# Two-layer encoder trunk on one core: neighbourhood-attention outputs laid out by features, with divided probabilities as the moving operand

## The chip, the core and the metric

The kernel runs on one core of a Trainium2 chip. The metric is device microseconds (us) of one execution of the whole program. A core has a matrix engine (TensorE, PE in the profile, with its weight loads as PEld), a vector engine (VectorE, DVE), a scalar engine (ScalarE, ACT), GpSimd (POOL) and a queue engine (SyncE, SP) that issues the transfers. The engines run at the same time, each in the order of its own program, and wait for each other through semaphores only.

## The reference

Two layers over 256 tokens of 1024 features. Each layer adds three parts to the residual: a mixer, a cross-attention into 256 memory tokens, and a gated convolutional feed-forward; each starts with an RMS norm. The change concerns the mixer and its output projection:

```python
proj = h @ w_in                         # q, k, v and gates of three groups of heads
ml_out = head_rms_norm(ml_h, ml_norm_g, ML_HEADS) * sigmoid(ml_o)      # 6 mLSTM heads
# 5 neighbourhood heads: 256 tokens on a 4 x 64 grid, window of 16 columns, all rows
s = einsum('brqhd,brkwhd->bhrqkw', qg, k_band) * d ** -0.5 + bias
s = where(in_win, s, -inf)
p = softmax(s)
o = einsum('bhrqkw,brkwhd->brqhd', p, v_band)
gla_out = head_rms_norm(gla_h, gla_norm_g, GLA_HEADS) * silu(g_g)      # 5 gated linear heads
return concatenate([ml_out, na_out, gla_out], axis=-1) @ w_out
```

Every head has 64 features. So of the 1024 mixed features, 384 come from mLSTM, 320 from the neighbourhood heads and 320 from gated linear attention (GLA). In blocks of 128 features (k = 0 to 7), blocks 0, 1 and 2 are mLSTM, 3 and 4 are neighbourhood, block 5 is half neighbourhood and half GLA, 6 and 7 are GLA.

## The kernel before, in words

Tokens lie on partitions in two tiles of 128 (`t`), features in eight blocks of 128 (`k`). All large products are made of three products of two parts: each weight and activation is split into an upper part (`whi`, `xhi`, `yhi`, written by ScalarE) and a lower part (`wlo`, `xlo`, `ylo`, written by VectorE), and `split_mm` (lines 663 to 667) issues upper by upper, upper by lower and lower by upper. Weights come in units of 1 MB or less through a ring of three slots: SP loads a unit into `raw` when the lower part of the unit three before it is done, ScalarE copies the upper part (`split_hi`, line 1096), VectorE subtracts for the lower part (`split_lo`, line 1455), and TensorE waits for it (`have`). Each engine takes the units in the one order of `layer_units`, at the places in its program where a `split_hi` or `split_lo` stands.

PSUM has eight banks. `layer_events` writes out by hand in which order TensorE fills which bank (`job`), and `layer_drains` in which order ScalarE and VectorE empty them. `free(name)` on TensorE waits until the job that had the bank before has been drained.

The neighbourhood stage is the loop over `hh` in 0 to 6, written three times, once in the program of each engine. For a head n:

- `nas`: TensorE multiplies queries by keys into a bank (line 882). Heads come in pairs (0, 1), (2, 3) at hh = 0 and 2, head 4 alone at hh = 4; the two heads of a pair lie in the two halves of the partitions.
- VectorE adds the bias with the window mask, negated, and takes the extreme of each row (line 1624), into `np_[:, n % 2]`.
- ScalarE takes the exponential, with the row sum in `nsum` (line 1262), and counts up `np_ready`.
- `nat`: one step later, TensorE waits for `np_ready` and transposes the four 128x128 blocks (line 864); ScalarE copies them to `npt[:, n % 2]` (line 1249).
- `nao`: again one step later, TensorE multiplies: the transposed exponentials stand, the 64 values of the head move, four products per head, tokens on the output partitions (line 872). VectorE inverts the row sums (line 1611) and scales the outputs by them into `tmb` (line 1614).

Between these, TensorE has fills: `gg` (gates of GLA) at hh = 0, then the cross-attention's key blocks `xk0` to `xk3`, two halves each (`NA_FILL`). In layer 1 two of the four key blocks are made elsewhere, so its fills are half as long. Each key block needs its split, and the first of them the eight upper and lower parts of the memory. VectorE's program of this loop also holds: the sum of the mLSTM heads over their two directions with its denominators (lines 1632 to 1638), the key splits, the products of GLA's queries and keys with their decays (lines 1646, 1647, 1655), the squares of the mLSTM heads (1588, 1589) and the split of `xv0a`.

Behind the loop comes GLA: `kt0` and `kt1` (turns of decayed keys, lines 900 and 904), `ga`, `kv`, then the memory's values `xv0`, `go` and `xv1a`. When `tmb` holds all mixed heads (`mixed_ready`), TensorE transposes the eight blocks (`mx_0` to `mx_3`, two blocks each, line 978), ScalarE and VectorE split them into `yhi` and `ylo` with the gains (lines 1301 and 1710), and TensorE makes the output projection (`wo0`, `wo1`), for each half unit first token tile 0, then tile 1. Token tile rows within the neighbourhood heads' blocks are stored in reversed order inside each grid row, and `mixed_parts` names which pieces of a block must be read backwards.

## Time and profile before

| | us |
|---|---|
| median of 3 runs | 879.58 |
| lowest and highest of them | 879.28, 880.8 |
| profiled execution, its time | 878.24 |
| profiled execution, its span | 876.3 |
| TensorE busy in the span | 861.8 |
| VectorE busy in the span | 596.0 |
| ScalarE busy in the span | 496.1 |

The span is that of the instructions on the core; the time also has what lies around it, 1.94 us here. Rows of a timeline give the start, the duration, the engine and line, the operands by name (arena is a region that holds the stages' temporaries, bank is PSUM) and how many like instructions are merged in the row. A bracket at the end says how long the engine stood idle before and what released it. Matrix products overlap: the next starts before the one before ends, so the step between starts is what one costs. A product of full 32-bit operands shows as two records, a transpose as one.

### The profile page before, as it was taken

The page shows a single profiled execution, that of the slowest core. Times are in us where ns is not written, and L with a number is a line of the kernel's source. Part 1 is how long each engine was busy: PE and PEld are TensorE (multiplying, and loading weights), DVE is VectorE, ACT ScalarE, POOL GpSimd, SP SyncE. Part 2 cuts the span into 40 slices and gives each one's busy share as a digit, 9 for nine tenths or more (in the row PEclk, how much of TensorE's full clock was granted, in tenths as well). Part 3 has the DMA queues.
Part 4 walks back from the last instruction along what each step waited for, and adds up shares of the span by engine and source line. Part 5 has one row for each costly group of instructions (what it writes and reads, how often), then busy time and mean ns, then how long its engine had stood idle before and what let it go on. Part 6 is the DMA issues. An engine that isn't in the chain of part 4 may idle for free.

```text
span 876.3 us, 14948 instructions
## 1 busy us (share of the span) xinstructions
PE 861.8 (98%) x6338; PEld 798.1 (91%) x6338; DVE 596.0 (68%) x820; ACT 496.1 (57%) x689; POOL 14.3 (2%) x35
## 2 busy tenths in 40 slices
PE   8999999999999999999999999999999899999997
PEld 8999998889889999999999999988898899999996
DVE  6887678757657666666577885887665666656655
ACT  7954663658647445445567546745755645445444
POOL 5000000000000000000000000000000000000000
PEclk9999999999999999999999999999999999999999
DMA  9735452364255555555448254335435365555541
GB/s 329 201 102 177 156 178 103 112 226 144 97 193 190 195 190 195 192 191 194 145 140 257 72 171 165 127 115 192 135 109 191 127 212 190 193 196 190 192 169 48
DMA packets 114665, 146.78 MB, mean 168 GB/s; under 512 B 10600, under 2 KB 94760, under 8 KB 114600
## 3 DMA queue, kind: packets, MB, share of 16 engines
q1 hardware_dynamic: 114456, 145.57, 49.7%
q8 instruction: 50, 0.82, 0.4%
q10 hardware_dynamic: 144, 0.26, 0.1%
q14 instruction: 15, 0.12, 0.0%
HBM read 144.77 MB, written 1.05 MB: 166 GB/s over the span
## 4 chain that ended last, share of the span: by engine, by line
PE 92%; ACT 3%; DVE 3%; issue 1%; DMA 0%; ACTq 0%; DVEq 0%
PE bank L665 26%; PE bank L666 25%; PE bank L667 25%; PE bank L706 4%; PE bank L743 2%; PE bank L832 2%; DVE wlo L1455 2%; PE bank L1017 2%; ACT whi L1096 1%; ACT yhi L1119 1%; PE bank L872 1%; PE bank L762 1%; PE bank L849 1%; DVE ylo L1710 1%; PE bank L882 1%
## 5 line engine op out<-in xcount | busy, mean ns | idle before, releaser
L1455 DVE TENSOR_TENSOR wlo<-raw,whi 128x2048 fp32r<-128x2048 f32 (+3 forms) x144 | 306.2, 2133 | 106.1 <-ACT whi L1096 105.2
L1096 ACT ACTIVATE whi<-raw 128x2048 fp32r<-128x2048 f32 (+3 forms) x144 | 257.4, 1793 | 53.5 <-PE bank L667 48.4
L665 PE MATMUL bank<-yhi,whi 128*128 128x256 f32 x704 | 195.1, 277 | 0.5 <-DVE ylo L1471 0.5
L666 PE MATMUL bank<-ylo,whi 128*128 128x256 f32 x704 | 194.6, 276 | 0.0
L667 PE MATMUL bank<-yhi,wlo 128*128 128x256 f32 x704 | 194.6, 276 | 0.0
L665 PEld LDWEIGHTS bank<-yhi,whi 128*128 128x128 f32 x704 | 132.2, 188 | 1.6 <-issue 0.7
L666 PEld LDWEIGHTS bank<-ylo,whi 128*128 128x128 f32 x704 | 132.2, 188 | 0.8
L667 PEld LDWEIGHTS bank<-yhi,wlo 128*128 128x128 f32 x704 | 132.2, 188 | 0.0
L665 PE MATMUL bank<-xhi,whi 128*128 128x256 f32 x320 | 91.4, 286 | 2.2 <-DVE wlo L1455 1.2
L665 PE MATMUL bank<-whi,xhi 128*128 128x512 f32 (+2 forms) x256 | 90.1, 352 | 0.0
L667 PE MATMUL bank<-xhi,wlo 128*128 128x256 f32 x320 | 88.9, 278 | 0.0
L666 PE MATMUL bank<-xlo,whi 128*128 128x256 f32 x320 | 88.8, 278 | 0.0
L667 PE MATMUL bank<-whi,xlo 128*128 128x512 f32 (+2 forms) x256 | 88.5, 346 | 0.0
L666 PE MATMUL bank<-wlo,xhi 128*128 128x512 f32 (+2 forms) x256 | 88.5, 346 | 0.0
L666 PE MATMUL bank<-wlo,fhi 128*128 128x512 f32 x176 | 69.0, 392 | 0.0
L665 PE MATMUL bank<-whi,fhi 128*128 128x512 f32 x176 | 68.9, 391 | 0.0
L667 PE MATMUL bank<-whi,flo 128*128 128x512 f32 x176 | 68.6, 390 | 0.0
L665 PEld LDWEIGHTS bank<-xhi,whi 128*128 128x128 f32 x320 | 60.3, 188 | 7.1 <-issue 5.2
L1395 ACT ACTIVATE arena<-bank,pcols 128x256 f32<-128x256 f32 x44 | 22.4, 561 | 67.1 <-PE bank L667 67.1
L667 PEld LDWEIGHTS bank<-xhi,wlo 128*128 128x128 f32 x320 | 60.1, 188 | 0.0
L666 PEld LDWEIGHTS bank<-xlo,whi 128*128 128x128 f32 x320 | 60.1, 188 | 0.0
L665 PEld LDWEIGHTS bank<-whi,xhi 128*128 128x128 f32 x256 | 48.1, 188 | 5.1 <-issue 1.3
(268 smaller groups left out, 1373.1 us busy)
## 6 DMA issues: line engine op xcount, KB each, us to landing
raw<-in_w_up SPq DMA_DIRECT2D x44, 1024.0 KB, 5.0
raw<-in_w_down SPq DMA_DIRECT2D x22, 1024.0 KB, 4.8
raw<-in_w_in SPq DMA_DIRECT2D x10, 1024.0 KB, 7.3
raw<-in_w_xk SPq DMA_DIRECT2D x8, 1024.0 KB, 5.1
raw<-in_w_xv SPq DMA_DIRECT2D x8, 1024.0 KB, 4.9
raw<-in_w_out SPq DMA_DIRECT2D x8, 1024.0 KB, 4.8
raw<-in_w_xq SPq DMA_DIRECT2D x8, 1024.0 KB, 5.7
raw<-in_w_xo SPq DMA_DIRECT2D x8, 1024.0 KB, 4.9
```

The lines of the kernel that those rows point to most:

```text
L665: mm(o, s_hi, m_hi, start=first, stop=False, skip_group_check=True)
L666: mm(o, s_hi, m_lo, start=False, stop=False, skip_group_check=True)
L667: return mm(o, s_lo, m_hi, start=False, stop=last, skip_group_check=True)
L706: last = mm(bank(name, 2, T)[:, f, :], w[:, k, f * P:f * P + P], x[:, k, :], start=k + i + f == 0, stop=k == KT - 1 and i == 2, skip_group ...
L743: last = mm(bank(names[t])[:, 0:n], x[:, k, t * P:(t + 1) * P], w[:, k, :], start=k + i == 0, stop=False, skip_group_check=True)
L762: last = nc.tensor.transpose(turned_bank(l, group, k)[:, t * P:(t + 1) * P], tmb[:, t, k * P:(k + 1) * P], ident[:])
L832: last = mm(o[:, t, d, :], w[:, c:c + P], mv[:, jt, g, :], start=i == 0, stop=i == len(src) - 1)
L849: last = mm(bank(f"mls{hh + x}", TT, T)[:, jt, :], qk[r, 3 + j, jt * P:(jt + 1) * P], qk[r, j, :], start=True, stop=True)
L1017: last = mm(bank(f"xo_{hh}", 2, T)[:, f, :], xv[:, jt, hh * XD + f * P:hh * XD + (f + 1) * P], xpt[:, hh, jt, :], start=jt == 0, stop=jt == 1)
L1096: A(weight(whi, gu), raw[:, gu % RING, 0:SIZE[gu]], ACT.Copy).then_inc(hi_done, 1)
L1395: last = A(fy[:, p % 2, f, :], bank(f"fa{p}", 2, T)[:, f, :], ACT.Identity, scale=pcol[:, RA + RB_W + 22 + j:RA + RB_W + 23 + j], bias=pco ...
L1455: tt(weight(wlo, gu), raw[:, gu % RING, 0:SIZE[gu]], weight(whi, gu), ALU.subtract).then_inc(lo_done, 1)
```

## The change

The neighbourhood outputs are computed with features on the partitions. The 64 values of a head stand and the transposed probabilities of all 256 queries move, two products per head. The heads of a pair (`NA_PAIRS`: 0 with 1, 2 with 3, 4 alone) go to the two halves of one bank's partitions. Outputs are made at three places instead of five (`NA_OUT`, hh = 3, 5, 6), before the turn of that step.

Since queries now lie along the free dimension, the division by the row sums can no longer be done on the outputs. VectorE divides the exponentials in `np_` itself (`shares_of`), between ScalarE's exponential and TensorE's turn, and the turn waits for a new semaphore `npn_ready`. The outputs are already turned, so they are split at once: ScalarE copies the upper part to `yna_hi`, VectorE subtracts for `yna_lo` (`heads_lo`); these arrays lie where the neighbourhood queries and keys were. The transposes of blocks 3 and 4 before the output projection go, and `yhi` and `ylo` are formed for six blocks instead of nine pieces (`MIXED_K`; of block 5 only its GLA half). The output projection starts with block 3 for both token tiles, then blocks 0, 1, 2, then the rest.

On VectorE the order inside the loop changes: the mLSTM head sums move from hh = 0 to hh = 2 (before the divisions of heads 2 and 3 in layer 0, behind them in layer 1), the GLA products stand behind the divisions, the split of the second key block (`xk1` in layer 0, `xk3` in layer 1) moves into hh = 0. On ScalarE that block's upper part moves before the draining of `gg1`, and the two GLA exponentials move behind the exponentials of heads 2 and 3. The drain of `nao2` stands behind those of `kt0` and `kt1`. The core of the diff:

```diff
+        if h in NA_OUT:
+            p = NA_OUT.index(h)
+            job(f"nao{p}", 4 + p % 2)
...
-        if h >= 2:
-            job(f"nao{h - 2}", 4 + (h - 2) % 2)
...
+NA_OUT = (3, 5, 6)
+NA_PAIRS = ((0, 1), (2, 3), (4,))
+NA_K = range(3, 6)
...
                 for hh in range(NAH + 2):
+                    if hh in NA_OUT:
+                        p = NA_OUT.index(hh)
+                        is_drained(pe, l, f"nat{NA_PAIRS[p][-1]}")
+                        free(f"nao{p}")
+                        for jt in range(TT):
+                            for g in NA_PAIRS[p]:
+                                r = slice(64 * (g % 2), 64 * (g % 2) + 64)
+                                last = mm(bank(f"nao{p}")[r, 0:T], nav[:, jt, g * DH:(g + 1) * DH], npt[:, g % 2, jt].rearrange("p a b -> p (a b)"),
+                                          start=jt == 0, stop=jt == 1, skip_group_check=True)
+                        last.then_inc(te_done, 1)
                     if 1 <= hh <= NAH:
                         g = hh - 1
-                        pe.wait_ge(np_ready, NAH * l + g + 1)
+                        pe.wait_ge(npn_ready, NAH * l + g + 1)
                         free(f"nat{g}")
...
                             for jt in range(TT):
-                                last = nc.tensor.transpose(bank(f"nat{g}", TT, TT, P)[:, t, jt, :], np_[:, g % 2, t, jt * P:(jt + 1) * P], ident[:])
-                        last.then_inc(te_done, 1)
-                    if hh >= 2:
-                        g = hh - 2
-                        is_drained(pe, l, f"nat{g}")
-                        free(f"nao{g}")
-                        for t in range(TT):
-                            for jt in range(TT):
-                                last = mm(bank(f"nao{g}")[:, t * DH:(t + 1) * DH], npt[:, g % 2, t, jt, :],
-                                          nav[:, jt, g * DH:(g + 1) * DH], start=jt == 0, stop=jt == 1)
+                                last = nc.tensor.transpose(bank(f"nat{g}", TT, TT, P)[:, jt, t, :], np_[:, g % 2, t, jt * P:(jt + 1) * P], ident[:])
                         last.then_inc(te_done, 1)
...
                     for k in (i, i + 4):
+                        if k not in MIXED_K:
+                            continue
                         for t in range(TT):
...
                     last.then_inc(te_done, 1)
-                for n in range(2):
-                    tm_unit(f"wo{n}", (f"wo{n}0", f"wo{n}1"), 512, "mx", n == 0)
+                tm_half("wo0", "a", ("wo00", "wo01"), 512, "mx", True, ks=(3,), first=3, ends=None)
+                tm_half("wo0", "a", ("wo00", "wo01"), 512, "mx", True, ks=(0, 1, 2), first=3, ends=2)
+                tm_half("wo0", "b", ("wo00", "wo01"), 512, "mx", True)
+                tm_unit("wo1", ("wo10", "wo11"), 512, "mx")
...
                 for hh in range(NAH + 2):
+                    if hh in NA_OUT:
+                        p = NA_OUT.index(hh)
+                        r = slice(0, 64 * len(NA_PAIRS[p]))
+                        is_filled(act, l, f"nao{p}")
+                        A(forwards(yna_hi[r, p, :]), backwards(bank(f"nao{p}")[r, 0:T]), ACT.Copy).then_inc(na_hi_ready, 1)
                     if 1 <= hh <= NAH:
...
                         drain(A(npt[:, (hh - 1) % 2].rearrange("p a b c -> p (a b c)"), bank(f"nat{hh - 1}"), ACT.Copy))
-                    if hh == 1:
-                        if l == 0:
-                            split_hi("xk1")
-                        else:
-                            split_hi("xk3")
-                        act.wait_ge(bc_ready, l + 1)
-                        A(b1[:], zc, ACT.Exp, scale=1.0 / 16).then_inc(eb_ready, 1)
-                        A(b3[:], zc, ACT.Exp, scale=-1.0 / 16).then_inc(eb_ready, 1)
                     if hh < NAH and hh % 2 == 0:
...
                             last.then_inc(np_ready, 1)
+                    if hh == 2:
+                        act.wait_ge(bc_ready, l + 1)
+                        A(b1[:], zc, ACT.Exp, scale=1.0 / 16).then_inc(eb_ready, 1)
+                        A(b3[:], zc, ACT.Exp, scale=-1.0 / 16).then_inc(eb_ready, 1)
                     if hh == 0:
...
+                        split_hi("xk3" if l else "xk1")
...
                 split_hi("wo0b")
-                for k in range(KT):
+                for k in MIXED_K:
                     is_filled(act, l, f"mx_{k % 4}")
-                    if k >= 4:
+                    if k - 4 in MIXED_K:
                         lo_is(act, l, "mx", k - 4)
-                    for r, v in mixed_parts(k):
-                        last = A(forwards(yhi[r, k, :]), v(turned_bank(l, "mx", k)[r, :]), ACT.Copy, scale=pcol[r, R_MG + k:R_MG + k + 1])
-                    last.then_inc(xhi_ready, 1)
+                    r, hi, _ = mixed(k)
+                    A(hi, turned_bank(l, "mx", k)[r, :], ACT.Copy, scale=pcol[r, R_MG + k:R_MG + k + 1]).then_inc(xhi_ready, 3 if k == 5 else 1)
                 split_hi("wo1b")
...
+                def heads_sum():
+                    is_drained(dve, l, f"mlo{MLH - 1}")
+                    dve.wait_ge(em_ready, l + 1)
+                    hr = hraw[:].rearrange("p t d h e -> p (t d h) e")
+                    link(stt(den[:, :], hr[:, :, DH], -1.0, hr[:, :, DH], ALU.mult, ALU.max))
+                    link(tt(den[:, :], den[:, :], em[:].rearrange("p t d h -> p (t d h)"), ALU.max))
+                    link(V.reciprocal(den[:, :], den[:, :]))
+                    link(tt(hr[:, :, 0:DH], hr[:, :, 0:DH], den[:].rearrange("p (n o) -> p n o", o=1).broadcast_to([P, 24, DH]), ALU.mult))
+                    link(tt(mlh, hraw[:, :, 0, :, 0:DH], hraw[:, :, 1, :, 0:DH], ALU.add))
+                def shares_of(g):
+                    dve.wait_ge(np_ready, NAH * l + g + 1)
+                    link(V.reciprocal(nsum[:, 2 * g:2 * g + 2], nsum[:, 2 * g:2 * g + 2]))
+                    for t in range(TT):
+                        last = ts(np_[:, g % 2, t, :], np_[:, g % 2, t, :], nsum[:, 2 * g + t:2 * g + t + 1], None, ALU.mult)
+                    last.then_inc(npn_ready, 1)
+                def heads_lo(p):
+                    dve.wait_ge(na_hi_ready, 3 * l + p + 1)
+                    r = slice(0, 64 * len(NA_PAIRS[p]))
+                    drain(tt(forwards(yna_lo[r, p, :]), backwards(bank(f"nao{p}")[r, 0:T]), forwards(yna_hi[r, p, :]), ALU.subtract))
                 for hh in range(NAH + 2):
-                    if hh == 2:
-                        dve.wait_ge(eb_ready, 2 * l + 2)
-                    if hh >= 2:
-                        g = hh - 2
-                        dve.wait_ge(np_ready, NAH * l + g + 1)
-                        link(V.reciprocal(nsum[:, 2 * g:2 * g + 2], nsum[:, 2 * g:2 * g + 2]))
-                        is_filled(dve, l, f"nao{g}")
-                        for t in range(TT):
-                            last = ts(tmb[:, t, ML + g * DH:ML + (g + 1) * DH], bank(f"nao{g}")[:, t * DH:(t + 1) * DH],
-                                      nsum[:, 2 * g + t:2 * g + t + 1], None, ALU.mult)
-                        drain(last)
                     if hh < NAH and hh % 2 == 0:
...
                         split_lo("ggb")
-                        is_drained(dve, l, f"mlo{MLH - 1}")
-                        dve.wait_ge(em_ready, l + 1)
-                        hr = hraw[:].rearrange("p t d h e -> p (t d h) e")
-                        link(stt(den[:, :], hr[:, :, DH], -1.0, hr[:, :, DH], ALU.mult, ALU.max))
-                        link(tt(den[:, :], den[:, :], em[:].rearrange("p t d h -> p (t d h)"), ALU.max))
-                        link(V.reciprocal(den[:, :], den[:, :]))
+                        for g in NA_PAIRS[0]:
+                            shares_of(g)
                         split_lo("xk2" if l else "xk0")
                         memory_lo("mem", l, range(KT))
-                        link(tt(hr[:, :, 0:DH], hr[:, :, 0:DH], den[:].rearrange("p (n o) -> p n o", o=1).broadcast_to([P, 24, DH]), ALU.mult))
-                        link(tt(mlh, hraw[:, :, 0, :, 0:DH], hraw[:, :, 1, :, 0:DH], ALU.add))
-                    if hh == 1 and l == 0:
-                        split_lo("xk1")
+                        split_lo("xk3" if l else "xk1")
                     if hh == 2:
+                        if l == 0:
+                            heads_sum()
+                        for g in NA_PAIRS[1]:
+                            shares_of(g)
                         if l:
-                            split_lo("xk3")
+                            heads_sum()
+                        else:
+                            split_lo("xk2")
+                        dve.wait_ge(eb_ready, 2 * l + 2)
                         is_drained(dve, l, "gk")
...
                         link(ins)
-                        if l == 0:
-                            split_lo("xk2")
                     if hh == 3:
...
                             split_lo("xk3")
+                        heads_lo(0)
                     if hh == 4 and l == 0:
...
                     if hh == 4:
+                        shares_of(4)
                         split_lo("xv0a")
-                    if hh == 5 and l:
-                        head_squares(mlh, sq, 0, MLH)
+                    if hh == 5:
+                        if l:
+                            head_squares(mlh, sq, 0, MLH)
+                        heads_lo(1)
                 is_filled(dve, l, "kt0")
...
                 drain(V.tensor_copy(kty[:].rearrange("p a b c -> p (a b) c"), bank("kt1", 4, P)[:, :, 0:32]))
+                heads_lo(2)
                 for i in range(4):
```

Not shown: the order of drains, which follows the above, the allocations, and `tm_half`, which gets the arguments `first` and `ends` and takes its inputs from `operand`, that is from `yna_hi` and `yna_lo` for blocks 3 to 5.

## Rows read from the trace of the kernel before

**Rows 1.** The page: busy time of each engine; granted clock in 40 slices

```profile
PE 861.8 (98%) x6338; PEld 798.1 (91%) x6338; DVE 596.0 (68%) x820; ACT 496.1 (57%) x689; POOL 14.3 (2%) x35
...
PEclk9999999999999999999999999999999999999999
```

**Rows 2.** Timeline of VectorE, layer 1: start us, us, line, names, count [idle before]

```profile
542.44 0.19 DVE L1632 SCALAR_TENSOR_TENSOR den<-arena 128x24 f32<-128x24 f32 x1
...
544.45 2.29 DVE L1455 TENSOR_TENSOR wlo<-raw,whi 128x2048 fp32r<-128x2048 f32 x1 [1.26 <-ACT whi L1096]
...
549.83 1.75 DVE L1637 TENSOR_TENSOR arena<-arena,den 128x1536 f32<-128x1536 f32 x1
...
553.40 0.17 DVE L1611 RECIPROCAL nsum<-nsum 128x2 f32<-128x2 f32 x1 [0.83 <-ACT arena L1257]
...
554.00 0.41 DVE L1624 CUSTOM_DVE_ANT_0 arena<-bank,bt 128x256 f32<-128x256 f32 x1
...
555.38 2.29 DVE L1455 TENSOR_TENSOR wlo<-raw,whi 128x2048 fp32r<-128x2048 f32 x1
...
557.58 0.68 DVE L1646 TENSOR_TENSOR arena<-gq,arena 128x512 f32<-128x512 f32 x1
...
560.10 0.17 DVE L1611 RECIPROCAL nsum<-nsum 128x2 f32<-128x2 f32 x1
...
560.69 1.28 DVE L1655 TENSOR_TENSOR arena<-arena 128x512 f32<-128x512 f32 x2
...
567.25 0.95 DVE L1588 TENSOR_TENSOR qk<-qk 128x768 f32<-128x768 f32 x1
...
569.10 0.15 DVE L1611 RECIPROCAL nsum<-nsum 128x2 f32<-128x2 f32 x1
```

**Rows 3.** Timeline of TensorE, layer 0, neighbourhood stage, in the same columns

```profile
114.25 1.00 PE L872 MATMUL bank<-nav,arena 128*128 128x64 f32 x8
115.18 1.13 PE L882 MATMUL bank<-nak,naq 64*128 64x256 f32 x8
116.25 0.38 PE L665 MATMUL bank<-xhi,whi 128*128 128x256 f32 x1
...
122.44 1.00 PE L872 MATMUL bank<-nav,arena 128*128 128x64 f32 x8
123.26 0.36 PE L665 MATMUL bank<-xhi,whi 128*128 128x256 f32 x1
...
130.18 1.13 PE L882 MATMUL bank<-nak,naq 64*128 64x256 f32 x4
131.24 0.38 PE L665 MATMUL bank<-xhi,whi 128*128 128x256 f32 x1
```

**Rows 4.** Timeline of TensorE, layer 0, carried GLA products

```profile
152.28 1.52 PE L956 MATMUL bank<-arena 128*64 128x256 f32 x12
```

**Rows 5.** Timeline of TensorE, layer 0, turning of the mixed heads and output projection

```profile
165.00 1.91 PE L978 MATMUL bank<-ident,tmb 128*128 128x128 f32 x16
166.77 0.47 PE L665 MATMUL bank<-whi,yhi 128*128 128x512 f32 x1
...
172.09 0.39 PE L667 MATMUL bank<-whi,ylo 128*128 128x512 f32 x1
172.79 0.50 PE L665 MATMUL bank<-whi,yhi 128*128 128x512 f32 x1 [0.32 <-DVE wlo L1455]
```

**Rows 6.** Timeline of VectorE, layer 0, one division of the cross-attention

```profile
217.70 0.62 DVE L1746 TENSOR_SCALAR tmb<-tmb,nsum 128x256 f32<-128x256 f32 x2
```

**Rows 7.** Timeline of ScalarE, layer 1, neighbourhood stage

```profile
546.79 1.71 ACT L1124 ACTIVATE xhi<-memT,pcols 128x256 fp32r<-128x256 f32 x4 [0.19 <-PE bank L667]
...
549.51 1.91 ACT L1096 ACTIVATE whi<-raw 128x2048 fp32r<-128x2048 f32 x1
...
554.80 0.51 ACT L1262 ACTIVATE arena<-arena,nmax 128x256 f32<-128x256 f32 x1 [1.00 <-DVE nmax L1624]
```

**Rows 8.** Timeline of TensorE, layer 1, first GLA turn

```profile
568.18 0.61 PE L900 MATMUL bank<-ident,arena 128*128 128x128 f32 x4
```

More of the change, by code:

```diff
@@ L521, in forwards, with operand, mixed @@
             return v.rearrange("p (r c) -> p r c", c=GW)
-        def mixed_parts(k):
-            lo, hi = k * P, k * P + P
-            return [(slice(max(lo, a) - lo, min(hi, b) - lo), v)
-                    for a, b, v in ((0, ML, forwards), (ML, ML + NA, backwards), (ML + NA, DM, forwards)) if max(lo, a) < min(hi, b)]
+        def operand(group, k):
+            if group == "mx" and k in NA_K:
+                return yna_hi[:, k - 3, :], yna_lo[:, k - 3, :]
+            return tuple(x[:, k, :] for x in PAIR[group])
+        def mixed(k):
+            r = slice(64, P) if k == 5 else slice(0, P)
+            return (r,) + tuple(x[r] for x in operand("mx", k))
+        MIXED_K = (0, 1, 2, 5, 6, 7)
         block = ctx.enter_context(nc.Block())
@@ L1706, in _ @@
                 split_lo("wo0a")
-                for k in range(KT):
+                for k in MIXED_K:
                     hi_is(dve, l, "mx", k)
-                    for r, v in mixed_parts(k):
-                        last = stt(forwards(ylo[r, k, :]), v(turned_bank(l, "mx", k)[r, :]), pcol[r, R_MG + k:R_MG + k + 1],
-                                   forwards(yhi[r, k, :]), ALU.mult, ALU.subtract)
-                    last.then_inc(xlo_ready, 1)
+                    r, hi, lo = mixed(k)
+                    stt(lo, turned_bank(l, "mx", k)[r, :], pcol[r, R_MG + k:R_MG + k + 1], hi, ALU.mult, ALU.subtract
+                        ).then_inc(xlo_ready, 3 if k == 5 else 1)
                 split_lo("wo1b")
```

32 lines of the change are left out of this document (22 added, 10 removed).

## The prediction

> **What bounds the kernel now.** I read the first part of the profile page first: TensorE is busy for 861.8 of 876.3 us, VectorE for 68% and ScalarE for 57% [rows 1]. TensorE sets the time almost everywhere, so the change is worth what it takes from TensorE's own work, less every wait that it puts in front of TensorE. The granted clock is at its upper level, 2.4 GHz, in all 40 slices [rows 1]. Then I read the timelines of TensorE, VectorE and ScalarE through the neighbourhood stage of both layers (about 99 to 139 us and 538 to 568 us) and through the turning of the mixed heads behind it, looking at start times: matmuls are pipelined, so the step from one start to the next is the price, not the duration printed. The reader should see in them that TensorE goes from group to group without a gap while VectorE has only small ones: in layer 1 its work runs through with one idle of 1.26 and one of 0.83 in 16 us [rows 2]. VectorE is thus the second limit of this stage, and the change lengthens just the chain that runs through it.
>
> **Change, TensorE's work.** A head's outputs now cost 0.93 or 0.82 us (114.25 to 115.18, 122.44 to 123.26), five heads per layer [rows 3]: 4.3 us at 0.86 each. The new form makes two pairs and a single head, 256 columns moving, 64 features stationary, the heads of a pair in the two halves of the output partitions. The nearest rows are the score products: two heads of 256 columns in the two row halves take 1.07 us (115.18 to 116.25), and one head alone takes 1.06 (130.18 to 131.24), so halves run beside each other and a single head wastes one [rows 3]. The carried GLA products have exactly the new form, halves alternating: 12 records in 1.52 us, or (1.52 - 0.38)/11 = 0.104 each, 0.83 for eight [rows 4]. Bounds for a pair are 0.83 below and 2 x 1.06 = 2.12 above (no overlap). I take 1.07, since those eight records enter and leave the half-array form once each, as a pair will. Per layer: 2 x 1.07 + 1.06 = 3.2, a saving of 1.1 if nothing waits.
>
> The Trainium skill (TensorEngine Tiling, Key Properties) says that changing the tiling mode drains the engine, and the change adds such switches. It agrees with the single head's 1.06 for four records; by that rule 0.83 is too low and 1.07 stands. By the same page's advice to swap the operands and tile the columns (When to Use Tiling) the products would halve, to about 2.2 us per layer, an estimate that would take 1 us more per layer if no wait came instead.
>
> **Change, turning and output projection.** Four of 16 transposes go per layer; 16 take 166.77 - 165.00 = 1.77 us, so 0.44 goes [rows 5]. Then TensorE waits at the second half of `wo0`: the last record of the first half starts at 172.09, steps there are 0.23, but the next starts at 172.79 behind a `wlo` split, 0.47 late [rows 5]. VectorE can only begin that split after its nine `ylo` operations; six remain, about 0.4 each (as the 256-column steps in [rows 2]), so it comes 1.2 earlier plus what the earlier first transposes give, against a TensorE that comes 0.44 earlier. The wait goes. The six products of k = 3 that now come first have inputs ready long before and cover the turn of k = 0. In layer 1 the same pattern stands; I take the same. Saving 0.91 per layer, 1.82 in all. Less ScalarE work there (nine `yhi` become six) is hidden as now.
>
> **Change, the wait that is added.** The turn of a head (`nat`) waited for its exponentials; it now waits until VectorE has divided them. A division is a reciprocal (0.2 to the next start) and two scalings of 128x256, which take 0.62 together in the cross-attention [rows 6]: 0.73 per head in a run, 0.8 until it is ready. Removed are the ten small scalings of 128x64 from PSUM; added are three subtractions of 128x256 from PSUM per layer, 0.35 to 0.4 each by the bias step (four in 555.38 - 554.00 = 1.38 [rows 2]). For heads 0 and 1 the divisions fall into VectorE's idle 1.26 us before the next key split [rows 2] and cost nothing. For heads 2 and 3 I lay the new order end to end.
>
> Layer 0: scores 2, 3 start at 114.25 instead of 115.18 and end at 115.32. TensorE's key block and the turn of head 2 take 123.26 - 116.25 less the 0.82 of outputs, 6.19, and outputs 0 with 1 1.07: it asks for `xk2` at 122.6 [rows 3]. VectorE begins at 115.4: biases 1.38, head sums 3.5 (0.75 from 542.44 to the start of the idle before 544.45, and 2.74 from 549.83 to the idle before 553.40), two divisions 1.46, and only then the `xk2` split, 2.2 (555.38 to 557.58) [rows 2]. That ends at 124.0. TensorE starts `xk2` at 124.1, not at 123.26: +0.84. Behind it three heads' outputs (2.6) become a pair and a single (2.13): -0.47. Nothing else there binds by the same count. Layer 0's stage: +0.37.
>
> Layer 1: ScalarE forms the upper part of `xk3` right after the memory (546.79 + 1.61), then 1.8 [rows 7], so VectorE splits `xk3` from 550.3 to 552.5, earlier than now, and biases 2, 3 end at 553.9. The first exponential starts 0.80 after the first bias, two per head of 0.5 each [rows 7]: head 2 is divided by 555.1, head 3 by 556.1. Then head sums 3.5 (559.6), GLA products 2.52 (557.58 to 560.10), decayed keys 1.2, lower part of outputs 0, 1 0.4 (563.8), bias of head 4 0.7, its exponentials until 565.7, its division (566.4), the `xv0a` split 2.2 (568.6), squares 1.85 (567.25 to 569.10), lower part of outputs 2, 3 0.4: 570.85 [rows 2]. `kt0`, the first GLA turn, takes the bank of these outputs (bank 5) and must wait for that last step. It starts at 568.18 now [rows 8], and at 570.9 then: +2.7. On the way TensorE already waits at the turn of head 4 for the division at 566.4; that wait lies inside the 2.7. What is queued behind `kt0` on TensorE is the whole GLA stage, and since TensorE has no slack behind it [rows 1], nothing gives it back. In layer 0 the same last step is done at about 137, before TensorE comes to `kt0`, because the head sums stood earlier. SP loads a unit into a ring slot when a split has freed it; the two splits that come later (`xk2` in layer 0, `xv0a` in layer 1) free slots for `xv0b` and `wo0a`, which are used only behind the GLA products, so these loads cost nothing.
>
> **Sum.** +0.37 + 2.7 - 1.82 = +1.25 us. Against the profiled execution (876.3 span, 878.24 time) that is 879.5; that execution lies 1.34 below the median, and against the median 879.58 it is 880.8, or +0.14%. What the measurement cannot tell from no change is 0.2%, 1.76 us (877.8 to 881.3), so the forecast is a small loss inside it. Its own range is 879.8 to 882.0: the VectorE chain holds to some 0.7 us, the output products to 0.24 less.
>
> **Rivals.** (a) VectorE keeps up. If it were through 2.7 us sooner in layer 1 and 1.5 in layer 0, only savings would stay: -2 x 1.1 - 1.82 = -4.0, 875.6. For it speaks that VectorE is idle a third of the whole span; against it that these idles do not lie in this stretch. 7%. (b) Half of that: layer 0 waits as computed, layer 1 does not (it decides from the point where the lower part of outputs 2, 3 is done before TensorE reaches `kt0`): 0.37 - 1.1 - 1.82 = -2.55, 877.0. 10%. (c) Slower: the two heads of a pair do not overlap. Then the pair costs 2.12; outputs 0, 1 hide in layer 0's wait, layer 1's hide in its wait, and only layer 0's second pair shows, +1.05: 881.9. The GLA rows speak against it. 7%.
>
> (d) Slower by the clock. Two waits close together in layer 1, at the turn of head 4 and at `kt0`, leave TensorE mostly idle for some 5 us; if the granted clock fell to its lower level, 1.2 GHz, for as long again, 5 us of work would cost 5 more: 885.8. In the profile no slice stands below 9 tenths, the start-up with its waits included [rows 1]. 6%. The Trainium skill (TensorE: Matmul & The Clock Gate, HAM oscillation) describes such gaps lowering the clock; the traces shown have no gap as long, so they neither confirm nor exclude it here.
>
> **Chances and range.** The forecast has 0.70; about 0.49 of it lies within 0.2%, 0.20 above, the rest below. Faster: 0.07 + 0.10 + 0.01 = 0.18; same 0.49; slower: 0.20 + 0.07 + 0.06 = 0.33. The range 876.8 to 882.9 leaves out (a), (d) and little of the rest.
>
> **What would show it.** Right: in layer 0 TensorE idle for about 1.5 us before `xk2`, released by the `wlo` split; in layer 1 idle before the turn of head 4 (released by the division) and before `kt0` (released by the `yna_lo` subtraction), the latter starting some 2.7 us later relative to the layer's `nat0`; a pair's outputs taking 0.8 to 1.1 us; no wait left at `wo0`'s second half; twelve transposes instead of 16. Wrong: `kt0` or the turn of head 4 going on without a wait, the pair taking 2 us, a granted clock below full in layer 1's stage, or a wait in a stage that I have not laid out, such as the state products or the norm behind `wo1`.

## The result, and the profile after

The changed kernel takes 883.12 us (median of 12 runs, 879.91 to 885.85), the kernel before 879.52 (12 runs, 877.7 to 880.8). The ratio is 1.0035 with a 95% interval of 1.0021 to 1.0048: slower by 0.35%, some 3.1 us, where +1.25 was forecast. The profiled execution took 882.81 with a span of 880.8, 4.5 more than before.

First the page of the changed kernel, busy time and granted clock, against [rows 1]. TensorE's busy time is no shorter (862.1 against 861.8) although 48 records are gone, since some of its work ran at a lower clock, as shown below. The 40 slices still show no fallen clock: a slice of 22 us is too coarse for what follows.

```profile
PE 862.1 (98%) x6290; PEld 793.4 (90%) x6290; DVE 597.8 (68%) x820; ACT 495.8 (56%) x689; POOL 14.3 (2%) x35
...
PEclk9999999999999999999999999999999999999999
```

Next TensorE's waits after (what waits, released by, us in total, times, longest; issue means that the profile names no releaser). The turn of a head (L899) now waits for a division (L1650), and `kt0` (L926) waits too. Of the split waits (L684) 1.64 is `xk2` in layer 0; the one at `wo0` [rows 5] is gone.

```profile
PE bank L899 <- DVE arena L1650: 2.5, 1, 2.5
PE bank L684 <- DVE wlo L1486: 2.5, 2, 1.6
...
PE bank L926 <- issue: 0.5, 1, 0.5
```

Where the 4.5 us came from, by the starts of a few groups of TensorE in both timelines (first score product `nas`, `kt0`, first turn of the mixed heads `mx`, first turn for the norm behind `wo1`). The +1.78 ahead of `nas` lies at start-up, where the diff changes nothing; it comes up again below. The stretch with the -0.49 varies as much among the kernels of the experiments (346.0 to 346.9), which do the same there.

| stretch | before | after | more | forecast |
|---|---|---|---|---|
| start to `nas`, layer 0 | 99.25 | 101.03 | +1.78 | 0 |
| `nas` to `kt0`, layer 0 | 39.84 | 40.89 | +1.05 | +0.37 |
| `kt0` to `mx` | 25.91 | 25.96 | +0.05 | 0 |
| `mx` to the norm's turn | 27.01 | 25.84 | -1.17 | -0.91 |
| on to `nas`, layer 1 | 346.37 | 345.88 | -0.49 | 0 |
| `nas` to `kt0`, layer 1 | 29.80 | 32.70 | +2.90 | +2.7 |
| `kt0` to `mx` | 25.91 | 27.54 | +1.63 | 0 |
| `mx` to the norm's turn | 27.00 | 25.84 | -1.16 | -0.91 |
| on to the end | 255.21 | 255.12 | -0.09 | 0 |

Layer 0, TensorE after (start, us, engine and line, operands, count, idle before), against [rows 3]. A pair of heads goes from 122.91 to 123.93, 1.02; the single head from 140.91 to 141.92, 1.01. Before `xk2` TensorE stands idle for 1.64, until VectorE has its split. Behind this wait the granted clock stays at 1.00 (all three windows of 2 us from 124 to 130).

```profile
122.91 1.08 PE L890 MATMUL bank<-arena,nav 128*64 128x256 f32 x8
123.93 0.66 PE L899 MATMUL bank<-ident,arena 128*128 128x128 f32 x4
126.23 0.36 PE L684 MATMUL bank<-xhi,whi 128*128 128x256 f32 x1 [1.64 <-DVE wlo L1486]
...
140.91 1.08 PE L890 MATMUL bank<-arena,nav 128*64 128x256 f32 x4
141.92 0.65 PE L926 MATMUL bank<-ident,arena 128*128 128x128 f32 x4
```

The turning of the mixed heads in layer 0, against [rows 5]: twelve transposes in 1.23 instead of 16 in 1.77, and the first half of `wo0` runs into the second at a step of 0.23, without the idle that there was (0.47, and some 0.16 of slower steps behind it).

```profile
167.88 1.47 PE L1006 MATMUL bank<-ident,tmb 128*128 128x128 f32 x12
169.11 0.48 PE L684 MATMUL bank<-whi,yna_hi 128*128 128x512 f32 x1
...
174.45 0.39 PE L686 MATMUL bank<-whi,ylo 128*128 128x512 f32 x1
174.68 0.39 PE L684 MATMUL bank<-whi,yna_hi 128*128 128x512 f32 x1
```

Layer 1, VectorE after, against [rows 2]: the end of the chain, read downwards. Bias of head 4, 1.16 idle for its exponentials, its division, the `xv0a` split, two steps of squares (the first is shown), and only at 571.79 the lower part of outputs 2 and 3, which frees the bank for `kt0`. It ends at 572.20, and `kt0` starts at 572.30.

```profile
565.07 0.41 DVE L1666 CUSTOM_DVE_ANT_0 arena<-bank,bt 128x256 f32<-128x256 f32 x1
...
567.00 0.17 DVE L1648 RECIPROCAL nsum<-nsum 128x2 f32<-128x2 f32 x1 [1.16 <-ACT arena L1289]
567.20 0.62 DVE L1650 TENSOR_SCALAR arena<-arena,nsum 128x256 f32<-128x256 f32 x2
567.73 2.28 DVE L1486 TENSOR_TENSOR wlo<-raw,whi 128x2048 fp32r<-128x2048 f32 x1
569.93 0.95 DVE L1619 TENSOR_TENSOR qk<-qk 128x768 f32<-128x768 f32 x1
...
571.79 0.41 DVE L1656 TENSOR_TENSOR yna_lo<-bank,yna_hi 128x256 fp32r<-128x256 f32 x1
```

TensorE in the same stretch, against [rows 8]. The pair of heads 2 and 3 (eight records) stands at 564.29, ahead of the turn of head 4; the four records at 569.78, just ahead of `kt0`, are head 4's own outputs. What the reader is to see beside the two waits: the rest of `xk3` steps by 0.22 (568.58 to 568.80) where 0.114 is usual, head 4's outputs take 1.97 where a single head takes 1.08 (140.91 above), and the twelve records that make GLA's states at 575.18 take 2.86 to the next start.

```profile
564.29 1.08 PE L890 MATMUL bank<-arena,nav 128*64 128x256 f32 x8
567.87 0.70 PE L899 MATMUL bank<-ident,arena 128*128 128x128 f32 x4 [2.50 <-DVE arena L1650]
...
568.58 0.42 PE L685 MATMUL bank<-xlo,whi 128*128 128x256 f32 x1
568.80 0.41 PE L686 MATMUL bank<-xhi,wlo 128*128 128x256 f32 x1
...
569.78 1.97 PE L890 MATMUL bank<-arena,nav 128*64 128x256 f32 x4
572.30 0.63 PE L926 MATMUL bank<-ident,arena 128*128 128x128 f32 x4 [0.55 <-issue]
...
575.18 2.93 PE L956 MATMUL bank<-gv,arena 64*128 64x256 f32 x12
578.04 0.77 PE L967 MATMUL bank<-gv,arena 64*32 64x64 f32 x12
```

The same state products in the kernel before took 1.49:

```profile
571.04 1.57 PE L930 MATMUL bank<-gv,arena 64*128 64x256 f32 x12
572.53 0.53 PE L941 MATMUL bank<-gv,arena 64*32 64x64 f32 x12
```

Busy time by windows of 2 us there (after the engines' busy times: the granted clock, the DMA share, GB/s). TensorE works 0.13 us between 566 and 568; from 568 the granted clock falls to 0.59 and 0.56, stands at 1.00 again, and falls a second time behind the wait at `kt0`: 0.50 is the lower level, 1.2 GHz.

```profile
566.00:568.00 2.00, 0.13 (x1) 0.13 (x2) 0.97 (x4) 1.23 (x5) 0.00 (x0) 1.00 0.00 0
568.00:570.00 2.00, 2.00 (x11) 1.78 (x12) 2.00 (x2) 1.40 (x2) 0.00 (x0) 0.59 0.00 0
570.00:572.00 2.00, 1.75 (x4) 0.54 (x3) 1.97 (x4) 1.70 (x3) 0.00 (x0) 0.56 0.38 34
572.00:574.00 2.00, 1.70 (x36) 1.52 (x38) 1.24 (x4) 1.97 (x5) 0.00 (x0) 1.00 1.04 404
574.00:576.00 2.00, 2.00 (x66) 1.85 (x62) 1.77 (x6) 1.68 (x1) 0.00 (x0) 0.79 0.23 86
576.00:578.00 2.00, 2.00 (x10) 1.11 (x8) 2.00 (x2) 0.00 (x0) 0.00 (x0) 0.50 0.04 8
```

So the theory for the runs: the VectorE chain sets `kt0` of layer 1, and the waits that it makes on TensorE lower the clock, which costs again behind them. The rival: the bank of outputs 2 and 3 alone is the matter, or the second fall is chance.

### The profile page after: what moved, and what is told of

Its sections match the earlier page's. It is cut to its first block, busy times and chain, and to the rows that moved or that the text cites. A ratio compares the mean times of both kernels' runs of the same rounds, so it can differ in the third digit from the quotient of the medians.

```text
span 880.8 us, 14836 instructions
## 1 busy us (share of the span) xinstructions
PE 862.1 (98%) x6290; PEld 793.4 (90%) x6290; DVE 597.8 (68%) x820; ACT 495.8 (56%) x689; POOL 14.3 (2%) x35
## 3 DMA queue, kind: packets, MB, share of 16 engines
HBM read 144.77 MB, written 1.05 MB: 166 GB/s over the span
## 4 chain that ended last, share of the span: by engine, by line
PE 91%; DVE 4%; ACT 3%; issue 1%; DMA 0%; ACTq 0%; DVEq 0%
PE bank L684 25%; PE bank L685 25%; PE bank L686 25%; PE bank L725 4%; PE bank L768 2%; PE bank L857 2%; DVE wlo L1486 2%; PE bank L1047 2%; ACT whi L1126 1%; PE bank L874 1%; PE bank L787 1%; PE bank L991 1%; ACT yhi L1149 1%; PE bank L956 0%; PE bank L908 0%
## 5 line engine op out<-in xcount | busy, mean ns | idle before, releaser
L684 PE MATMUL bank<-yhi,whi 128*128 128x256 f32 x704 | 195.1, 277 | 0.5 <-DVE ylo L1502 0.5
L684 PEld LDWEIGHTS bank<-yhi,whi 128*128 128x128 f32 x704 | 132.2, 188 | 1.6 <-issue 0.7
L684 PE MATMUL bank<-xhi,whi 128*128 128x256 f32 x320 | 92.5, 289 | 3.4 <-DVE wlo L1486 2.5
L684 PE MATMUL bank<-whi,xhi 128*128 128x512 f32 (+2 forms) x256 | 90.1, 352 | 0.0
L684 PE MATMUL bank<-whi,fhi 128*128 128x512 f32 x176 | 68.9, 391 | 0.0
L684 PEld LDWEIGHTS bank<-xhi,whi 128*128 128x128 f32 x320 | 61.2, 191 | 8.4 <-issue 3.9
L684 PEld LDWEIGHTS bank<-whi,xhi 128*128 128x128 f32 x256 | 48.1, 188 | 5.2 <-issue 1.3
```

The lines of the kernel that those rows point to most:

```text
L684: mm(o, s_hi, m_hi, start=first, stop=False, skip_group_check=True)
```

## The experiments

All are edits of the changed kernel; each is compared with runs of the kernel before on the same chip. Each has one profiled execution, whose clock need not be that of its other executions. Where an expectation speaks of the outputs of heads 2 and 3 behind the turn of head 4, the row is that of head 4's outputs.

**e1_bank**, layer 1: the lower part of outputs 2, 3 ahead of the `xv0a` split and the squares.

```diff
                         shares_of(4)
+                        if l:
+                            heads_lo(1)
                         split_lo("xv0a")
...
-                        heads_lo(1)
+                        else:
+                            heads_lo(1)
```

> The changed kernel, but in layer 1 VectorE forms the lower part of outputs 2 and 3 (which frees the bank of kt0) right behind the division of head 4, ahead of the xv0a split and the squares. Theory W (VectorE's order makes the waits): kt0, counted from the layer's first score product, starts about 1.3 us earlier than the 32.7 us of the changed kernel, and the time falls by 1.0 to 2.0 us against the changed kernel (up to 3 if the granted clock then stays up). Rival N (the next wait takes its place: VectorE's copies of kt0 and kt1 still stand behind the split and the squares, so kv waits instead): kt0 earlier, kv not, time within 0.5 us of the changed kernel. Rival O (the half-array products are what costs, waits are a by-product): no change at all.

Measured: 880.48 (12 runs; before 879.77), ratio 1.0009 (0.9995 to 1.0023). `kt0` came 0.56 earlier, less than expected: the wait at the turn of head 4 stays, and behind it the rest of `xk3` and the outputs ran at the lower clock, so that they set `kt0`. Its wait went. The time fell more than that, by 0.26% or 2.3 us against the changed kernel's ratio (the intervals barely overlap); in the profile the stretch behind `kt0` gave another 1.53. TensorE of this run:

```profile
567.90 0.84 PE L899 MATMUL bank<-ident,arena 128*128 128x128 f32 x4 [2.41 <-DVE arena L1650]
...
569.96 1.90 PE L890 MATMUL bank<-arena,nav 128*64 128x256 f32 x4
571.78 0.66 PE L926 MATMUL bank<-ident,arena 128*128 128x128 f32 x4
...
574.69 1.57 PE L956 MATMUL bank<-gv,arena 64*128 64x256 f32 x12
576.18 0.53 PE L967 MATMUL bank<-gv,arena 64*32 64x64 f32 x12
```

The states' products behind it are back at 1.49. From the turn of head 4 to `kt0` it took 3.88 (567.90 to 571.78); where the clock stays up, the same work takes 2.35 (568.65 to 571.00 in e7 below). So without the bank's wait `kt0` could stand at about +30.6 at full clock, an estimate: the bank holds some 2.1 of the 2.9 us, and here the first fall of the clock took the place of 1.5 of them. Between these two profiled executions the second fall, behind `kt0`, came with the wait there and went with it.

**e2_key_split**, layer 0: `xk2` is split ahead of the head sums and the divisions of heads 2, 3.

```diff
+                    if hh == 1 and l == 0:
+                        split_lo("xk2")
                     if hh == 2:
...
-                        else:
-                            split_lo("xk2")
```

> The changed kernel, but in layer 0 the split of xk2 stands before the biases of heads 2 and 3, in VectorE's idle stretch of 2.1 us, instead of behind the head sums and the divisions. Theory W: TensorE's idle 1.64 us before xk2 goes, kt0 of layer 0 starts 1.3 to 1.9 us earlier (40.9 us behind the layer's first score product now), and the time falls by as much. Rival N: the xk3 split or the division of head 2 is late instead and TensorE waits there: under 0.5 us. Rival O: no change.

Measured: 882.91 (12 runs), ratio 1.0032 (1.0015 to 1.0048), so the time was missed. Layer 0 did what was expected: no wait for `xk2`, `kt0` at +38.77 from `nas` instead of +40.89. But in layer 1 of the profiled execution the clock stood at the lower level from 568 to 580 (two of its windows):

```profile
568.00:570.00 2.00, 1.96 (x5) 0.74 (x4) 1.97 (x3) 2.00 (x2) 0.00 (x0) 0.50 0.02 8
...
578.00:580.00 2.00, 2.00 (x19) 1.18 (x16) 0.83 (x2) 0.00 (x0) 0.00 (x0) 0.50 0.12 8
```

From `kt0` to the GLA outputs `go` it took 17.87 us there, where the kernel before takes 13.20: the gain of 2.1 in layer 0 was lost again in layer 1. Not every execution loses it: the profiled one is among the slow ones. Six of the twelve have a mean granted clock of 0.987 to 0.989 and took 884.88 in the mean, the other six, at 0.995, took 880.74, where the changed kernel's six at 0.995 took 881.83.

**e3_fill**: TensorE multiplies the identity in layer 1's two waits, into a bank that is free there. The results are not used.

```diff
                         g = hh - 1
+                        if l and g == 4:
+                            free("kt1")
+                            keep_clock(11, bank("kt1"))
                         pe.wait_ge(npn_ready, NAH * l + g + 1)
...
+                if l:
+                    keep_clock(9, bank("kt1"))
                 pe.wait_ge(qd_ready, l + 1)
                 free("kt0")
```

> The changed kernel with 11 identity products into a free bank before the turn of head 4 in layer 1 and 9 before kt0, work that TensorE does while it would wait. Waits and their releasers stay as they are. If the granted clock falls because TensorE stands idle in these two waits (rival d of the prediction), it now stays at its upper level through kt0 to kv, kt0 starts where it did, xv0 about 1.6 us earlier against it, and the time falls by 1.3 to 2 us. If the clock falls for another reason (the small products themselves, or the half-array form), the granted clock in that stretch stays at 0.5 to 0.8 and the time does not move by more than 0.5 us.

Measured: 880.97 (12 runs, 880.23 to 882.87), ratio 1.0019 (1.0007 to 1.003). TensorE of this run: the extra products fill both waits (563.59 and 568.49), head 4's outputs (567.48) take 1.08 again, `kt0` stands where it stood (+32.73), and the states' products take 1.50.

```profile
563.59 2.72 PE L664 MATMUL bank<-ident 128*128 128x128 f32 x22
...
567.48 1.08 PE L890 MATMUL bank<-arena,nav 128*64 128x256 f32 x4
568.49 2.27 PE L664 MATMUL bank<-ident 128*128 128x128 f32 x18
570.60 0.60 PE L931 MATMUL bank<-ident,arena 128*128 128x128 f32 x4
...
573.45 1.57 PE L961 MATMUL bank<-gv,arena 64*128 64x256 f32 x12
```

In the profile, work that does nothing gives back what the clock took: 13.19 us from `kt0` to `go` instead of 14.82. In the time the loss goes from 0.35% to 0.19%, near the 0.14% that was forecast for full clock; the two intervals overlap (1.0021 to 1.0048, 1.0007 to 1.003).

**e6_fill_turn** and **e7_fill_gla** cover one wait each: e6 has the first block of that diff alone, e7 the second (with the `free("kt1")` in it).

> The changed kernel with extra identity products only before layer 1's turn of head 4 (11 of them), the wait before kt0 left bare; nothing of the result changes. Theory A (the two waits close together make the clock fall): with one of them covered the granted clock stays at 1.00 from 562 to 580, kt0 at about +32.7, go at about +45.9, time near 881.0 as with both covered. Theory B (the wait before kt0 is enough by itself): the rest of xk3 and the outputs of heads 2, 3 run at full clock, but the granted clock is near 0.5 for some us behind kt0, go at +47 or later, time near 882.

> The changed kernel with extra identity products only before layer 1's kt0 (9 of them), the wait at the turn of head 4 left bare; nothing of the result changes. Theory A (it takes both waits): granted clock 1.00 throughout, time near 881.0. Theory B (the wait at the turn of head 4 is enough by itself): granted clock near 0.55 from 568 to 572 as in the changed kernel, the rest of xk3 takes 1.5 instead of 0.8 to 0.9 us and the outputs of heads 2, 3 about 2.5; kt0 hardly later, since it waits for VectorE anyway; the second fall behind kt0 may go, time between 880.5 and 882.5.

Measured on another chip (before 878.8): e6 883.78 (6 runs), ratio 1.0056 (1.0041 to 1.0071); e7 881.63 (8 runs), ratio 1.0027 (1.0015 to 1.0038). In e6 the clock falls behind the bare wait at `kt0`, and the states take 2.73 (574.05 to the next start):

```profile
570.79 0.63 PE L929 MATMUL bank<-ident,arena 128*128 128x128 f32 x4 [2.01 <-issue]
...
574.05 2.79 PE L959 MATMUL bank<-gv,arena 64*128 64x256 f32 x12
576.78 0.53 PE L970 MATMUL bank<-gv,arena 64*32 64x64 f32 x12
```

In e7 the bare wait at the turn of head 4 is as long as in the changed kernel, 2.50, but here the clock did not fall behind it, in this execution:

```profile
568.65 0.66 PE L899 MATMUL bank<-ident,arena 128*128 128x128 f32 x4 [2.50 <-DVE arena L1653]
...
569.99 1.08 PE L890 MATMUL bank<-arena,nav 128*64 128x256 f32 x4
571.00 2.27 PE L664 MATMUL bank<-ident 128*128 128x128 f32 x18
```

So one wait is enough for a fall (e6 behind `kt0`, e1 behind the turn), and it does not come in every execution. In e6 theory B held in the profile, but the time missed its 882 by 1.8: the profiled execution, 881.28, is the fastest of the six, and what the others lost (three have a mean clock of 0.991 to 0.994) no trace shows. In e7 neither theory held in full: no fall in the profile, as theory A said, but a time above that of both waits covered. Its two executions at a mean clock of 0.999 took 879.64 and 879.69, the six below 881.85 in the mean.

**e5_fill_key**: e2 and e3 together.

> The changed kernel with two edits: in layer 0 VectorE splits xk2 before the head sums and the divisions of heads 2 and 3, and in layer 1 TensorE runs 20 extra products of the identity in its two waits (11 before the turn of head 4, 9 before kt0, into a bank that is free there); nothing of the result changes. Theory (layer 0's wait for xk2 costs about 2 us, and the earlier run with the key split alone lost it again to the clock in layer 1): kt0 of layer 0 at about +38.8 us from its first score product, kt0 of layer 1 still at about +32.7 and go at about +45.9, granted clock 1.00 in layer 1's stage, time about 2.0 below the run with the extra products alone, near 878.9. Rival (the gain of layer 0 is lost again somewhere behind the neighbourhood stage, whatever the clock): the start of n2's turn in layer 0 not earlier, time near 881.

Measured: 880.23 (12 runs; before 878.8), ratio 1.001 (1.0002 to 1.0018): lower than e3's by 0.0009, some 0.8 us, where 2.0 was expected, and the intervals overlap. In the profile layer 0 came to the norm's turn 1.38 us earlier than in e3 (+90.89 against +92.27), and layer 1 kept its clock (13.18 from `kt0` to `go`). What the profile gained there it lost at start-up, where the granted clock fell from 28 to 32 us (0.66 and 0.50) and `nas` of layer 0 came 1.66 later than in e3 (101.26 against 99.60). Of its executions the four with a mean granted clock of 0.998 or more took 878.96 in the mean, e3's four 880.52. These are two chips: the kernel before, at 0.998 or more, took 878.59 in the mean on e5's (13 executions) and 879.28 on e3's (15). At a like clock e5 thus lies 0.4 above before and e3 1.2. So the profile shows the gain of layer 0, at a like clock some 0.9 us of it is left, and its size over all executions stays uncertain.

**e4_order**: the VectorE chain itself is shortened. Layer 0 as in e2. In layer 1 the denominators of the head sums go into VectorE's wait for head 4's exponentials; their division goes behind the division of head 4; their addition, the squares and the `xv0a` split go behind what TensorE waits for; ScalarE's root of the squares moves behind them, and the upper part of `xv1a` ahead of it.

```diff
                     if hh == 4:
+                        if l:
+                            heads_den()
                         shares_of(4)
-                        split_lo("xv0a")
+                        if l == 0:
+                            split_lo("xv0a")
                     if hh == 5:
                         if l:
-                            head_squares(mlh, sq, 0, MLH)
+                            heads_divided()
                         heads_lo(1)
+                        if l:
+                            heads_added()
...
                 heads_lo(2)
+                if l:
+                    split_lo("xv0a")
...
                 ins.then_inc(state_ready, 1)
+                if l:
+                    head_squares(mlh, sq, 0, MLH)
                 split_lo("xv1a")
```

> The changed kernel with VectorE's order rearranged in both layers: layer 0 as in the run with the earlier xk2 split; in layer 1 the denominators of the head sums stand in the wait for head 4's exponentials, the rest of the sums around the lower part of outputs 2 and 3, the xv0a split behind the copies of kt0 and kt1, the squares behind the GLA states, and on ScalarE the upper part of xv1a before the root of the squares. Theory W: the turn of head 4 and kt0 no longer wait, the clock stays up, kt0 of layer 1 starts 27.5 to 28.5 us behind the layer's first score product (32.7 in the changed kernel, 29.8 in the kernel before), and the time is 6 to 8 us below the changed kernel, 2.5 to 4.5 below the kernel before. Rival N (VectorE as a whole is too slow for this stage, whatever the order): the waits come back behind the stage, at kv, at the states or at the turn of the mixed heads, and the time is within 1 us of the kernel before or above. Rival O: no gain over the kernel before, since the products are no cheaper.

Measured: 875.54 (6 runs, 874.3 to 876.53), ratio 0.9946 (0.9928 to 0.9964): faster than both kernels, as theory W said. `kt0` of layer 1 stands at +28.29, 1.5 earlier than before the change. TensorE of this run goes from the outputs of heads 2 and 3 (563.76) to the states with no wait worth a mark; a short one, 0.21, comes back at `go`:

```profile
563.76 1.08 PE L890 MATMUL bank<-arena,nav 128*64 128x256 f32 x8
564.92 0.66 PE L899 MATMUL bank<-ident,arena 128*128 128x128 f32 x4
...
566.27 1.08 PE L890 MATMUL bank<-arena,nav 128*64 128x256 f32 x4
567.28 0.66 PE L926 MATMUL bank<-ident,arena 128*128 128x128 f32 x4
...
570.18 1.57 PE L956 MATMUL bank<-gv,arena 64*128 64x256 f32 x12
```

The stage of layer 1 in all nine profiled executions, us from its first `nas` and, last, from `kt0` to `go`:

| kernel | wait at `kt0` | `kt0` | `go` | `kt0` to `go` |
|---|---|---|---|---|
| before | none | 29.80 | 43.00 | 13.20 |
| changed | bare | 32.70 | 47.52 | 14.82 |
| e1_bank | none | 32.14 | 45.43 | 13.29 |
| e2_key_split | bare | 32.71 | 50.58 | 17.87 |
| e3_fill | covered | 32.73 | 45.92 | 13.19 |
| e5_fill_key | covered | 32.76 | 45.94 | 13.18 |
| e6_fill_turn | bare | 32.70 | 47.57 | 14.87 |
| e7_fill_gla | covered | 32.73 | 45.93 | 13.20 |
| e4_order | none | 28.29 | 41.90 | 13.61 |

Wherever TensorE stood bare in front of `kt0`, the stretch behind it took 14.8 to 17.9 us; wherever it was covered or did not wait, 13.2 to 13.6. Three kernels stand against six, with one profiled execution each. Length alone does not tell which wait does it: behind the turn of head 4, bare for 2.41 to 2.50 in four of them, the clock fell in three (changed, e1, e2) and not in e7; behind the bare wait at `xk2` in layer 0, 1.43 to 1.64 in five of them (changed, e1, e3, e6, e7), it stayed at 1.00 each time. The 0.55 at `kt0` of the changed kernel was shorter than those, but came 4 us behind the start of a first fall.

## Why the prediction was right, and where not

**The places and the mechanism** were right: slower, through waits of TensorE on a longer VectorE chain, at the three places named, and a smaller saving behind the turning. The size was off: +1.25 forecast, some +3.1 measured. With 0.35% the change left the 0.2% within which the forecast lay, and the median of 883.12 lies above the forecast's own range (879.8 to 882.0) and 0.2 above the wide one (to 882.9; the ratio times 879.58 gives 882.7). Point by point:

- **Output products.** 1.07 a pair and 1.06 a single were forecast; 1.02 and 1.01 it was. Rival (c), no overlap at 2.12, fell. The Trainium skill (TensorEngine Tiling (Array Packing), Key Properties) says that a change of tiling mode drains the engine. No run here shows that drain by itself. That a single head of half as many records costs as much as a pair shows only that the halves run beside each other, and so the single head's 1.06 was no sign of the drain in the prediction either. What the traces allow is an estimate: twelve records of the carried GLA products take 1.44 to 1.45 to the next start in all nine kernels, the pair's eight 1.02, so four more cost 0.43, and some 0.16 a group is left for entering and leaving.
- **Layer 0**, +0.37 forecast, +1.05 measured. The wait at `xk2` is 1.64 (forecast 1.5), the split ends 0.2 later than laid out, and `xk2` starts 0.35 later than forecast against `nas` (25.20 against 24.85). The other 0.33 lies behind it: the 256-column products ran 0.1178 apart for two stretches where they had run 0.1137 and 0.1145 before. That e2 got 2.1 back by the place of one split, 1.64 of it the wait, shows that the wait was the main cost.
- **Layer 1 up to `kt0`**, +2.7 forecast, +2.90 measured. The chain laid end to end held to 0.2 at each of its steps once the layer's later start of 1.22 is taken off: division of head 4 done 566.51 (forecast 566.4), split 568.71 (568.6), squares 570.57, last step 570.98 (570.85). It was put down to the bank of outputs 2, 3, which holds some 2.1 of it at full clock (the estimate at e1). But e1 showed that taking this wait away gives back only 0.56, since the clock falls behind the turn of head 4 all the same, which the forecast had not priced.
- **Turning and `wo0`**, -0.91 a layer forecast, -1.17 and -1.16 measured, both parts as said: 0.54 for four transposes (0.44), and the whole wait of 0.47 with the slower steps behind it (0.16), which the forecast had left out.
- **Rivals (a) and (b)**, no waits, fell; e4 shows what (a) was worth: 875.54 measured where (a) gave 875.6. That the two meet so closely is in part luck: in the profile `kt0` comes 0.78 earlier than before the change in layer 0 and 1.51 in layer 1, where (a) has 1.1 each, the turning gives 0.5 more than forecast, and 0.41 is lost again behind `kt0` of layer 1.
- **Behind `kt0`** the forecast had nothing, and this step failed: the sum priced all work at the upper clock and left the fall to rival (d) at 6%, on the ground that no slice of the page stood below 9 tenths. The changed kernel's page, with its falls, shows the same. The fall came, at the place that (d) names. Its price was too high: 1.63 in the profile instead of 5, for two reasons. The first fall (568 to 572) lies ahead of `kt0`, which waits for VectorE anyway (e3 holds the clock and has the same `kt0`); and the second lasts some 3 us. Over many executions the clock costs what e3 gets back: the ratio goes from 1.0035 to 1.0019, some 1.4 us, or 2.4 by the medians' distances to before (3.60 against 1.20), with intervals that overlap. What then stays, 0.19% (0.07 to 0.30), is near the forecast.

The Trainium skill (TensorE: Matmul & The Clock Gate, HAM oscillation) describes gaps of TensorE that lower the clock for the work behind them. The runs agree in that, but the gaps that sufficed here, 2.01 (e6) to 2.50 us (changed kernel), are shorter than those of which the section speaks. The same page (Part 1: The HAM clock gate) says that the number of products that one kernel runs at the lower clock as its work sets in varies from run to run. No run here counts that; the fall varies in a like way, with 2.41 idle in e1 and 2.50 in e7 at the same turn, a fall in one and none in the other.

Left open: the start-up. In six of the nine profiled executions, the changed kernel's among them, the granted clock fell between 28 and 33 us (0.76, 0.50 and 0.89 in the changed kernel's three windows), where the diff changes nothing; in those of before, e3 and e6 it did not. It costs the profile 1.78. Whether it comes more often in the changed kernel than in the one before was not measured. Some fall comes in executions of the kernel before too: of the 48 with a clock on record, 20 have a mean granted clock below 0.998 and are slower than the others by 1.2 us on one chip and 1.5 on the other. Where in the program, no trace shows.

## What to carry to other kernels

A step inserted between two engines is priced by the whole queue of the engine that does it: lay that queue end to end with measured durations, and move what nobody waits for behind what somebody waits for before judging the step (here 883.12 became 875.54). A wait on TensorE can cost more than its length: behind four of the five bare waits of 2.0 to 2.5 us here the clock fell, behind the five of 1.4 to 1.6 us in layer 0 it did not. So look at the granted clock in windows of 2 us, not in slices of the page. If the wait can't go, products of no use in it are worth trying: 20 of them gave back 1.63 in the profile and, with overlapping intervals, 1.4 to 2.4 us in the time.

## What was not expected of the hardware

**Spread as a sign of the clock.** The changed kernel's twelve executions lie within 5.9 us, before's twelve within 3.1, though 29 others of before span 5.2. The changed kernel's mean granted clock is 0.989 to 0.995: the six at 0.995 took 881.83 in the mean, the six below 884.31. In e3, with both waits covered, it is 0.995 to 0.999, and the four at 0.999 took 880.52.

**Two steps for the same product.** The fp32r products of 256 columns start 0.1135 to 0.1145 us apart in some stretches and 0.1177 to 0.1178 in others, with the clock at 1.00, and most stretches keep their step once it has set in (the first of layer 0, for `xk0`, lies between the two or above). Which stretch gets which differs between kernels: behind the first pair's scores 0.1178 before and 0.1135 after, behind the third turn's wait 0.1178 in the changed kernel and 0.1135 in e3. A stretch of 48 costs 0.2 us more at the slower step; the cause wasn't sought.
